# A two-slot weight ring and one held output slab per layer, in a two-layer decoder trunk

## The reference, cut to what matters

```python
for i in range(DEPTH):                                   # DEPTH = 2
    h = h + token_mixer(rms_norm(h, norm_mix_g[i]), positions, w_in[i], ...,  w_o[i])
    h = h + peer_ffn(rms_norm(h, norm_ffn_g[i]), peer_w_query[i], peer_sub_keys[i], peer_u[i], peer_v[i])
    h = h + per_layer_embedding(h, p[i], w_ple[i], ple_norm_g[i], w_ple_gate[i])
return rms_norm(h, final_norm_g)
```

## Time and profile before

| | us |
|---|---|
| median of 3 runs | 1580.63 |
| lowest and highest of them | 1579.78, 1587.18 |
| profiled execution, its own time | 1579.42 |
| its span in the profile | 1577.6 |

### The profile page before, as it was taken

One profiled execution on the slowest core, in us unless ns is written; L12 is line 12 of the kernel. 1 busy time (PEld: TensorE's weight loads), 2 busy tenths in 40 slices (PEclk: granted clock), 3 DMA queues, 4 the chain that ended last, 5 costly groups with the idle time before them and its releaser, 6 DMA issues.

```text
span 1577.6 us, 18210 instructions
## 1 busy us (share of the span) xinstructions
PE 1135.7 (72%) x6364; PEld 444.0 (28%) x6364; DVE 1068.1 (68%) x2691; ACT 563.5 (36%) x1781; POOL 585.5 (37%) x516
## 2 busy tenths in 40 slices
PE   7995577795658877776567886788556966677666
PEld 6771133260113522233112443335111311111112
DVE  3468987679986357666998536757899664554445
ACT  0503365232333246423233325633234333333331
POOL 0004444445442324433443333443445443433330
PEclk9995778997778978888768997898666976665767
DMA  8148999999999999999999999999999999999991
GB/s 350 55 193 361 421 411 408 404 405 421 421 421 384 420 420 420 420 422 419 422 420 408 416 418 420 387 414 413 417 421 420 372 422 421 420 421 421 422 421 75
DMA packets 91437, 613.25 MB, mean 389 GB/s; under 512 B 9936, under 2 KB 10448, under 8 KB 25808
## 3 DMA queue, kind: packets, MB, share of 16 engines
q0 software_dynamic: 73728, 536.90, 82.4%
q1 hardware_dynamic: 17616, 75.18, 11.9%
HBM read 610.99 MB, written 1.05 MB: 388 GB/s over the span
## 4 chain that ended last, share of the span: by engine, by line
DMA 34%; DVE 30%; PE 24%; ACT 7%; issue 3%; POOL 1%; DVEq 0%; POOLq 0%; ACTq 0%
DMA ring<-in_rows,ids 34%; DVE ring L1007 13%; PE acc L486 8%; PE bank L737 3%; PE bank L785 3%; PE bank L637 2%; PE bank L520 2%; DVE wb L1285 2%; DVE part_id L1337 1%; ACT diag L833 1%; ACT L828 1%; PE bank L772 1%; DVE top_i L1292 1%; ACT act_w L830 1%; POOL ring L460 1%
## 5 line engine op out<-in xcount | busy, mean ns | idle before, releaser
L486 PE MATMUL acc<-ring,diag 64*64 64x512 f32 x4096 | 707.4, 800 | 342.5 <-ACT diag L833 340.1
L460 POOL DMA_INDIRECT ring<-in_rows,ids x512 | 585.3, 1143 | 945.9 <-PE acc L486 777.8
L1007 DVE CUSTOM_DVE_ANT_0 ring<-ring,xc 128x1024 f32<-128x1024 f32 x512 | 616.6, 1223 | 377.7 <-DMA ring<-in_rows,ids 375.3
L828 ACT ACTIVATE gel<-pre 128x1 f32<-128x1 f32 x512 | 103.4, 202 | 830.2 <-DVE pre L1007 815.0
L486 PEld LDWEIGHTS acc<-ring,diag 64*64 64x64 f32 x4096 | 144.0, 161 | 857.4 <-ACT diag L833 748.0
L833 ACT ACTIVATE diag<-cst,act_w 128x64 f32<-128x64 f32 x512 | 178.1, 348 | 16.7
L830 ACT ACTIVATE act_w<-gate,gel 128x1 f32<-128x1 f32 x512 | 150.7, 294 | 16.7
L737 PE MATMUL bank<-hT,held 128*128 128x128 f32 x512 | 62.2, 282 | 7.6 <-DVE hT L1041 7.6
L737 PEld LDWEIGHTS bank<-hT,held 128*128 128x128 f32 x512 | 59.8, 196 | 17.8 <-DVE hT L1041 10.5
L637 PE MATMUL bank<-wring,hT 128*128 128x512 f32 x128 | 58.8, 603 | 5.2 <-DVE hT L1044 4.4
L785 PE MATMUL bank<-wring,hT 128*128 128x512 f32 x112 | 52.1, 610 | 0.7 <-DVE hT L1044 0.7
(11 more groups left out here) (236 smaller groups left out, 995.5 us busy)
## 6 DMA issues: line engine op xcount, KB each, us to landing
wring<-in_w_out SPq DMA_DIRECT2D x16, 1024.0 KB, 12.5
wring<-in_w_in SPq DMA_DIRECT2D x16, 978.0 KB, 9.8
wring<-in_w_gate SPq DMA_DIRECT2D x11, 1024.0 KB, 12.8
held<-in_w_query SPq DMA_DIRECT2D x8, 1024.0 KB, 12.3
ring<-in_rows,ids POOLq DMA_INDIRECT x512, 14.2
ring<-in_w_in SPq DMA_DIRECT2D x8, 978.0 KB, 15.2
wring<-in_w_latent SPq DMA_DIRECT2D x4, 768.0 KB, 9.6
wring<-in_keys SPq DMA_DIRECT2D x4, 512.0 KB, 11.2
```

The costliest lines, as they stand in the source:

```text
L460: pool.indirect_dma_start(out=ring[:, n % RING, :], out_offset=None, in_=rows, in_offset=bass.IndirectOffsetOnAxis(ap=ids[:, w % 2, k:k + ...
L486: last = pe.matmul(acc[rows_of(c), r, :], diag[rows_of(r), j, :], ring[rows_of(r), j, D:][:, cols_of(c)], start=False, stop=True, skip_gro ...
L828: act.activation(gel[:, j:j + 1], pre[:, j:j + 1], ACT.Gelu).then_inc(gelued, 1)
L1007: dve.tensor_tensor_reduce(out=u, in0=u, in1=xc[:, step % 2, :], scale=1.0, scalar=0.0, op0=ALU.mult, op1=ALU.add, accum_out=pre[:, j:j + ...
```

## The change

The ring `wring` has two slots; `held` has five. The fifth slot holds `out` slab 3 of a layer for both tiles, so `out` 3 leaves the ring and is loaded twice in all instead of four times. The loads into `held` (first `out` 3, then the four of `w_query`) are issued when SP comes to `out` 1 of the layer's first tile, no longer at `keys`. For the last gate, slabs 0 and 1 stay in the ring, and slabs 2 and 3 go to `held` slots 1 and 2. `out_half` now rises for both column halves of slab 3, and VectorE waits for it twice in the place of one wait on `weight_used`.

```diff
-WRING, WSLOT = 3, 2048
-HELD = KT // 2
+WRING, WSLOT = 2, 2048
+HELD = KT // 2 + 1
 KEPT = WRING
+OUT_HELD = KT // 2 - 1
...
-REST_LOADS = [("latent", 0)] + [("out", k) for k in range(KT // 2)] + \
+REST_LOADS = [("latent", 0)] + [("out", k) for k in range(OUT_HELD)] + \
              [("keys", 0)]
...
-                if (kind, k, t) == ("keys", 0, 0):
+                if (kind, k, t) == ("out", 1, 0):
                     if l:
                         sp.wait_ge(ids_ready, CHUNKS * TILES * l)
-                    for i in range(HELD):
-                        load(held[:, i, :].rearrange("p (a n) -> p a n", a=2), source["query"](l, i), held_in[i])
+                    load(slab(HELD - 1), source["out"](l, OUT_HELD), held_in[HELD - 1])
+                    for i in range(HELD - 1):
+                        load(slab(i), source["query"](l, i), held_in[i])
...
-                if (kind, k, s) == ("gate", 2, STEPS - 2):
+                if (kind, k, s) == ("gate", 1, STEPS - 2):
                     sp.wait_ge(query_ready, 2 * STEPS)
-                    load(held[:, 0, :].rearrange("p (a n) -> p a n", a=2), source["ple"](l, 0), held_in[0])
-                    load(held[:, 1, :].rearrange("p (a n) -> p a n", a=2), source["gate"](l, KEPT), held_in[1])
+                    load(slab(0), source["ple"](l, 0), held_in[0])
+                    for i in range(KEPT, KT // 2):
+                        load(slab(i - KEPT + 1), source["gate"](l, i), held_in[i - KEPT + 1])
...
-                w = weights()
+                l, t = layer_tile(s)
+                kept = k == OUT_HELD
+                if kept and t == 0:
+                    next_of(held_in[HELD - 1], 16)
+                w = held[:, HELD - 1, :] if kept else weights()
...
-                    if c == 0 and k == KT // 2 - 1:
+                    if kept:
                         last.then_inc(out_half, 1)
-                release(last)
+                if not kept:
+                    release(last)
...
-                        if i == 2 and c == 0:
+                        if i == 2:
                             next_of(out_half)
-                        elif i == 2:
-                            wait_products(dve, "out", s, slab)
```

More of the change, by code:

```diff
@@ L413, in _, with slab @@
             }
+            def slab(i):
+                return held[:, i, :].rearrange("p (a n) -> p a n", a=2)
             for n, (kind, k, s) in enumerate(order):
@@ L795, in embed @@
                         if kept:
-                            next_of(held_in[1], 16)
-                        w = held[:, 1, :] if kept else weights()
+                            next_of(held_in[k - KEPT + 1], 16)
+                        w = held[:, k - KEPT + 1, :] if kept else weights()
                         last = gate(0, k, w)
@@ L802, in embed @@
                         if kept:
-                            last.then_inc(gate_half, 1)
+                            if k == KT // 2 - 1:
+                                last.then_inc(gate_half, 1)
                         else:
@@ L811, in embed @@
                             next_of(hT_ready)
-                        w = wring[:, (len(order) - KEPT + k) % WRING, :] if k < KEPT else held[:, 1, :]
+                        w = wring[:, (len(order) - KEPT + k) % WRING, :] if k < KEPT else held[:, k - KEPT + 1, :]
                         last = gate(c, k, w)
```

## The result

The changed kernel takes 1589.2 us (median of 13 runs, 1583.6 to 1593.6); the kernel before took 1580.8 us beside it (13 runs, 1574.1 to 1587.2). The ratio is 1.0041, with a 95% interval of 1.0027 to 1.0055: **4 to 9 us slower** (the two medians alone give 1.0053, in the interval too). The forecast was 1575.9 us, 5 us faster. The median lies just inside the given range of 1571 to 1590, but the sign is wrong.

What follows compares the result with a forecast made beforehand. The prediction took the DMA engines' bytes at about 420 GB/s as the bound from window 0 on. 1579.4 - 5.2 + 0.5 = 1574.7 us for the profiled execution; the median, 1.2 us above, gave 1575.9, range 1571 to 1590.

Steps and rivals of the forecast that it cites:

- bytes term: Out slab 3 loaded twice instead of four times, in windows 0 and 2: 2.10 MB less, a gain of 5.2 us.
- What bounds the kernel: From window 0 on, time is bytes divided by about 420 GB/s, plus DMA loss where nothing is outstanding.
- shares of 0.96 and 0.95: DMA shares around the starts of windows 1 and 3, over 43 and 53 us, read as 4.4 us unused.
- Rival 3: More than the bytes comes back, the 4.4 us unused at window starts: 1571.0 us, chance 0.12.
- The shorter ring: Later loads of out, in and gate slabs make TensorE wait about 40 us more, in 12 waits.
- What hides it: Gathers outstanding keep the DMA engines busy during TensorE's weight waits, so these cost 0.5 us, within bounds of 0 and 26.
- 5.7 gathers in flight: While TensorE waits for a weight: 14.2 us to landing over 2.5 us of engine time each; 14 us to run out.
- rival 1: Waits for out 2, gate and in, windows 0 to 2, reach the DMA engines: 1601.8 us, half about 1589; chance 0.15.
- Nothing for TensorE itself: The forecast took the matmuls as unchanged and gave TensorE no term beyond its waits for weights.
- Held loads moved ahead: Out 3 and four query loads issued before out 1, in startup and layer 1: cost nothing, no term.

Runs made afterwards that it cites:

- bytes_only: The kernel before, three slots; second tiles multiply by query slab 0 instead of loading out slab 3, so not the reference's result: ratio 0.9959, 6.5 us faster.
- late_out1: The kernel before, three slots, where SP waits one release longer before one load, out slab 1 of step 1: ratio 1.0025, 3.9 us slower.
- narrow_gate: The kernel before, three slots, where SP waits one release longer before gate slabs 1 to 3 of steps 0 and 1: ratio 1.0018, 2.8 us slower.
- burst_only: The kernel before, three slots, with the four query loads issued at out 2 of the first tile: ratio 1.0020, 3 us slower, medians 0.9997.
- gate_held: The changed kernel with ple and gate slabs 1 to 3 of step 0 loaded early into held query slots: ratio 1.0069 to the kernel before.

## Why the prediction was wrong

The bytes term held. The step that failed is the +0.5 us for the shorter ring: ring_only, which has the short ring and nothing else, is 12 us slower (7 to 17; by its medians 6). That is more than the saving of 5 to 6.5 us. The parts, in the order of the prediction:

1. **What bounds the kernel**: right, but taken too evenly. The windows are paced by the DMA engines except where TensorE sets the pace with the row ring full, and it is there that the change acts. I read shares of 0.96 and 0.95 as a small loss at window starts. They were the sign of such places, and the GB/s of the same rows, 388 and 384 against 421, stand for nearly twice the loss that the shares do (8.0 us for 4.4). Rival 3 said that nothing in the edit touches the start of a window. It does: gate slab 1, ready in the ring when the window began, is now loaded inside it.
2. **Bytes removed, -5.2 us**: the term is right for what it names; bytes_only gave -6.5 (3.5 to 9.6). **What it leaves out is a part of the failed step**: I counted what leaves windows 0 and 2 and not what the shorter ring moves between windows. The third slot let SP load out slab 1 of step 1 in the startup, where the third slice of the earlier trace rows shows 193 GB/s. With two slots it falls into window 0. late_out1 prices that at 3.9 us (1.6 to 6.2), more than half of the saving. Gate slab 1 of step 0 leaves window 0 at the same time, so window 0 is shorter by one slab's 2.5 us on balance (5.5 and 6.1 us were measured in two profiles), and the loss shows in windows 1 and 2.
3. **The shorter ring, 12 waits and 40 us**: right, 12 and 40.7 us. The times to landing and the distances between release and need carried well, though the largest single wait (7.8 us, in slab 2) had a load of 0.5 MB ahead of it in SP's queue that I had not counted.
4. **"What hides it", 0.5 us**: right for `in` and `out`. 20.0 us of `in` waits cost 1.7 us (up to 4.1) and 14.7 us of `out` waits about 1, by an estimate that the intervals leave wide. The front stretches of windows 1 and 2, where the `in` waits are, have 2.1 and 1.5 us unused for 0.3 and 0.4 before. Wrong for the gates. The count of 5.7 gathers in flight is a mean; from 472 to 488, as window 1 begins, GpSimd stands 15.4 us with no gather issued, and a gather lands in 14.2. So by the first gates the ring is as good as full of landed rows (VectorE waits for rows only 6.2 us between 470 and 520), and the argument that a wait of 5 us lets two gathers land has nothing to stand on. narrow_gate is 2.8 us slower (0.3 to 5.2), and in its profile that is a balance: 11 us more in windows 1 and 2 together against 5.5 us less in window 0. This is rival 1, at the place it named and in a quarter of its waits; I gave it 0.15.
5. **Nothing for TensorE itself.** A wait also slows what follows it. In the changed kernel's window 2 (TensorE's time line):

```profile
880.47 1.95 PE L492 MATMUL acc<-ring,diag 64*64 64x512 f32 x16
886.05 6.74 PE L796 MATMUL bank<-wring,hT 128*128 128x512 f32 x8 [3.63 <-DMA wring<-in_w_gate]
892.71 1.95 PE L492 MATMUL acc<-ring,diag 64*64 64x512 f32 x16
```

   After 3.63 us of waiting the slab takes 6.74 us; the gate slabs before it take 3.70. So this wait held TensorE up by 6.7 us and not 3.6, and the gate stretch around it is 6.0 us longer than before. The `out` slabs after their waits take 6.63, 5.33 and 6.34 us for 3.70 as well, in stretches where it cost little.
6. **Held loads moved ahead, "no term"**: the startup part held; no load was late there. For the burst of layer 1 the reason was wrong. "The DMA engines are full in both" stretches was true of the kernel before because the burst was in one of them: with it gone, the output and query stretches of window 1 lost 4.5 and 2.5 us in two profiles, and 0.1 with the burst back. The estimates of the runs are 1.4 us (inside the noise) and 3 us (nothing by the medians), so a cost in time is likely and not shown.

Together, in % of the time: bytes -0.41; out slab 1 +0.25; gates +0.18; `in` +0.11; the rest of the ring +0.06; burst +0.1 to +0.2. The sum is +0.3 to +0.4, and 0.41 was measured. With the intervals of its terms the sum is known to about 0.4 either way, so the agreement proves little; that the ring costs more than the bytes give back is shown, its division into parts is an estimate, best supported for out slab 1 and the gates. ring_only by itself came out higher than its parts (0.77 for 0.60), so the ring's share may be larger than this list has it.

What stays open: why burst_only is slower with no more unused time than before, and the scatter of single profiles in the gate stretches (10.9 to 16.4 us unused in kernels that differ only in when the queries are loaded), which makes any one profile a weak witness for 3 us.

## What to carry to other kernels

In a kernel that the DMA engines bound, ask of each megabyte not only how often it is moved but when. In this one it was free in the startup, and while TensorE set the pace with every buffer full; elsewhere it cost its full time. So a prefetch slot can be worth more than the waits it saves, by what it lets cross from a full stretch to an empty one (late_out1), and loading earlier can cost (gate_held). And a wait is covered only if something is still outstanding at that moment; look there, not at the mean number in flight.

## What the runs showed of the hardware

TensorE's waits had a second price, in the granted clock. Around the wait that ends at 886 in the changed kernel (third number from the end: the clock): just before it, in it, and twice 2 us after it.

```profile
880.00:882.40 2.40, 2.40 (x18) 0.51 (x16) 1.23 (x2) 1.52 (x3) 0.54 (x1) 1.00 1.04 434
882.40:886.00 3.60, 0.01 (x2) 0.00 (x0) 0.00 (x0) 0.00 (x0) 1.63 (x2) 0.91 1.01 422
886.00:888.00 2.00, 1.95 (x3) 0.92 (x4) 0.00 (x0) 0.00 (x0) 0.00 (x0) 0.50 1.03 432
888.00:890.00 2.00, 2.00 (x4) 0.92 (x3) 0.00 (x0) 0.06 (x1) 0.00 (x0) 0.50 1.01 422
```

TensorE was busy at 1.00 until 882.4, then idle for 3.6 us, and came back at 0.50: 1.2 GHz in place of 2.4. The slab that took 6.74 us for 3.70 ran at that level for most of its time. The kernel before had 0.96 over its whole gate stretch, and the changed one 0.86. The DMA engines follow late, as rows of 10 us show:

```profile
880.00:890.00 10.00, 6.37 (x23) 2.36 (x22) 1.23 (x2) 1.57 (x4) 2.18 (x2) 0.77 1.02 427
890.00:900.00 10.00, 5.22 (x23) 1.75 (x22) 7.25 (x20) 3.45 (x6) 2.69 (x2) 0.84 1.00 366
900.00:910.00 10.00, 10.00 (x73) 5.45 (x75) 7.48 (x14) 5.07 (x18) 5.36 (x4) 0.88 0.69 256
```

They still move 427 GB/s during the wait and fall to 256 only 20 us on. Between the two, GpSimd stands for slots that TensorE has not freed, and issues no gather until 894:

```profile
894.10 0.94 POOL L466 DMA_INDIRECT ring<-in_rows,ids  x1 [9.77 <-PE acc L492]
```

The kernel before moves 417 to 425 GB/s from 873 to 903, at the same place of the window. The lost time shows in another place than its cause.
